# A two-layer encoder kernel: three places for expert tiles and four for gathered rows, in place of four and three

## What is computed

```python
def peer_ffn(h, w_query, sub_keys, expert_u, expert_v):     # 8 heads, 128 x 128 keys
    q = (xc @ w_query).reshape(PEER_CHUNK, PEER_HEADS, 2, PEER_HALF)
    sc = jnp.einsum('chpd,hpkd->chpk', q, sub_keys)
    ...                                   # top 16 of each half, then top 16 of the 256 pairs
    gate = jax.nn.softmax(top_s, axis=-1)
    u = jnp.take(expert_u, idx, axis=0)   # 128 experts for each token, 2048 floats each
    act = jax.nn.gelu(jnp.einsum('chkd,cd->chk', u, xc), approximate=False)
    vsel = jnp.take(expert_v, idx, axis=0)
    return jnp.einsum('chk,chkd->cd', (gate * act).astype(xc.dtype), vsel)
```

## Time and profile before

| | us |
|---|---|
| median of 3 runs | 3923.73 (3920.32 to 3927.78) |
| the profiled execution, its own time | 3927.2 |
| its span, first to last instruction | 3925.3 |
| TensorE busy | 3732.7 (95%) |
| VectorE busy | 2349.7 (60%) |
| GpSimd busy | 1168.9 (30%) |
| U tiles of the first layer | from 775.9 |
| V tiles of the first layer | 1389 to 1952 |
| U tiles of the second layer | from 2731 |
| V tiles of the second layer | 3345 to 3908 |

### The profile page before, as it was taken

One profiled execution on the slowest core, in us unless ns is written; L12 is line 12 of the kernel. 1 busy time (PEld: TensorE's weight loads), 2 busy tenths in 40 slices (PEclk: granted clock), 3 DMA queues, 4 the chain that ended last, 5 costly groups with the idle time before them and its releaser, 6 DMA issues. The chain is left out here.

```text
span 3925.3 us, 63110 instructions
## 1 busy us (share of the span) xinstructions
PE 3732.7 (95%) x26656; PEld 3403.6 (87%) x26656; DVE 2349.7 (60%) x4219; ACT 429.9 (11%) x1020; POOL 1168.9 (30%) x924
## 2 busy tenths in 40 slices
PE   7997889999999999999979978899999999999998
PEld 5786784799999899999967867747999998999998
DVE  5975752696388754444369657516953886544442
ACT  1013220110111000000010222101101110000000
POOL 2610000023133355455335100000331333555553
PEclk9998899999999999999989978999999999999999
DMA  5430013489899999999643300143998999999995
GB/s 160 139 119 10 2 45 134 141 340 405 334 397 396 392 368 357 373 349 372 241 138 130 118 10 2 45 160 129 359 399 336 398 397 390 379 364 368 349 359 228
DMA packets 305655, 994.14 MB, mean 253 GB/s; under 512 B 58861, under 2 KB 157549, under 8 KB 223917
## 3 DMA queue, kind: packets, MB, share of 16 engines
q0 software_dynamic: 118656, 587.71, 38.8%
q1 hardware_dynamic: 186720, 402.41, 28.0%
HBM read 1071.38 MB, written 2.10 MB: 273 GB/s over the span
## 5 line engine op out<-in xcount | busy, mean ns | idle before, releaser
L1679 PE MATMUL bank<-ycT,ex_tile 128*128 128x160 f32 x8192 | 1134.6, 300 | 0.0
L1679 PEld LDWEIGHTS bank<-ycT,ex_tile 128*128 128x128 f32 x8192 | 1119.9, 191 | 8.7 <-issue 8.4
L1752 PEld LDWEIGHTS bank<-ex_W,ex_tile 128*128 128x128 f32 x8192 | 1113.3, 190 | 6.7 <-issue 6.7
L1752 PE MATMUL bank<-ex_W,ex_tile 128*128 128x160 f32 x8192 | 1116.6, 299 | 0.0
L1618 POOL DMA_INDIRECT ex_row<-in_peer_u,ex_rows x240 | 260.5, 1085 | 1639.7 <-DVE ex_rows L1912 1191.8
L1954 DVE CUSTOM_DVE_ANT_0 ex_row<-ex_row,ex_h_wide 128x2048 f32<-128x2048 f32 x192 | 439.1, 2291 | 387.8 <-DMA ex_row<-in_peer_u,ex_rows 385.2
L1960 DVE SCALAR_TENSOR_TENSOR ex_sums<-ex_row,ex_weight,ex_sums 128x2048 f32<-128x2048 f32 x186 | 437.1, 2350 | 368.0 <-DMA ex_row<-in_peer_v,ex_rows 368.0
L336 PE MATMUL pj_bank<-pj_hT,pj_piece 128*128 128x256 f32 x2048 | 461.1, 384 | 5.9 <-DVE pj_hT L607 5.9
L1629 POOL DMA_INDIRECT ex_tile<-in_peer_v,ex_wanted x256 | 326.7, 1276 | 452.0 <-PE bank L1752 421.3
L336 PEld LDWEIGHTS pj_bank<-pj_hT,pj_piece 128*128 128x128 f32 x2048 | 389.6, 192 | 72.3 <-issue 13.8
L799 PE MATMUL bank<-arena,ycT 128*128 128x512 f32 x512 | 222.4, 593 | 2.0 <-PEq L884 2.0
(11 more groups left out here) (377 smaller groups left out, 3326.5 us busy)
## 6 DMA issues: line engine op xcount, KB each, us to landing
ex_tile<-in_peer_uT SPq DMA_DIRECT2D x256, 1024.0 KB, 8.1
pj_piece<-in_w_in SPq DMA_DIRECT2D x32, 2048.0 KB, 8.7
arena<-in_w_out SPq DMA_DIRECT2D x16, 2048.0 KB, 7.9
query_w<-in_peer_w_query SPq DMA_DIRECT2D x16, 1024.0 KB, 5.5
ex_row<-in_peer_u,ex_rows POOLq DMA_INDIRECT x312, 9.6
ex_row<-in_peer_v,ex_rows POOLq DMA_INDIRECT x256, 8.9
ex_tile<-in_peer_v,ex_wanted POOLq DMA_INDIRECT x256, 8.0
x<-in_x SPq DMA_DIRECT2D x1, 2048.0 KB, 8.8
```

What stands on the lines that cost most here:

```text
L1679: mm = mmul(o, ring[:, j % SLOTS, k * P:k * P + P], hT[k // 4][:, k % 4, 0:DENSE], start=(k == 0), stop=(k == KT - 1))
L1752: mm = mmul(bank[:, at_, lo:lo + DENSE], ring[:, i % SLOTS, m * P:m * P + P], W[:, j, :], start=(j == 0 and m % 3 == 0), stop=(j == TILES ...
```

## The change

One place moves from the ring of tiles to the ring of rows; the sum of both stays at seven, so all else in the on-chip memory lies where it lay. `FOLD_1_AT` moves by two.

```diff
-SLOTS = 4
-RING = 3
+SLOTS = 3
+RING = 4
-WIDEN_2, FOLD_1, FOLD_1_AT = 28, 64, 147
+WIDEN_2, FOLD_1, FOLD_1_AT = 28, 64, 149
```

## The result

| | before | after |
|---|---|---|
| median of 4 runs, us | 3925.8 (3920.3 to 3928.7) | 3996.7 (3988.2 to 4002.0) |
| profiled execution, its span | 3925.3 | 3993.0 |

The changed kernel takes 1.018 of the time before (95% interval 1.0168 to 1.0192), 71 us more by the medians. It is slower, as forecast, and the time lies inside the range, 1.3 us from its upper end, but the loss is more than twice the 33 us of the sum. One number further down needs a note: of ten runs of the kernel with VectorE's lists later, one took 15348 us; it has no trace, and the ratio leaves it out.

A forecast was written before the change was run, and what follows sets the result against it. TensorE was taken as the bound at 4.35 us a tile, DMA engines right behind. Terms V +30, U +5, turn +6, fold -8 sum to +33 us, forecast 3957 us; range 3930 to 3998.

The forecast's parts named there:

- the V term: V tiles of both layers: landings over 7.75 us make TensorE wait with three places; +30 us, between 0 and 81.
- its signs: Profile after: short L1752 waits, V stretch over 563 us, DMA share below 0.96, fold waits about 4 shorter, first V issue later.
- turn: From U to V tiles: v_tile(0) issued some 5 us later behind two more gathers; 3 us a layer, +6 together.
- fold: U tiles 114 to 117: fourth row place puts VectorE one row further ahead; 4 us a layer, -8 together.
- SyncE's loop: SyncE issuing U tiles in laps of three in place of four: some more branches, costing nothing.
- U tiles 0 to 61: U tiles with gathers: landings over the 8.30 us limit make TensorE wait; +5 us, range 0 to 12, both layers.
- U tiles 104 to 113 and 118 to 127: Late U tiles: 1.3 us from tile 104, taken in by the fold's wait, costing nothing unless that wait goes.
- (4.51 + issue + landing) / 3: Time per tile with three places, or 4.35 us if more; V landings up to 7.75 us cost nothing.
- the rival's half: First rival's fold part: fourth row lets VectorE reach the fold in time, winning all 21.7 us; whole rival 3902, chance 0.07.
- the first two rivals: Landings shrink under the limit: fold's wait goes, 3902 us, chance 0.07; or fold gives one turn, 3927 us, chance 0.08.
- The third: Four rows queue in front of a V tile, so landings grow by one us: 4065 us, chance 0.08.
- The fourth: Fourth place for rows never filled when it matters, so the -8 is missing: 3965 us, inside the forecast.

The follow-up runs named there:

- e1: Changed kernel with the fourth place for rows taken away (three places for tiles, three for rows): 4009.6 us, ratio 1.0212 to the kernel before.
- e2: Changed kernel with 92 in place of 94 gathers ahead of the first V tile: 3985.1 us, ratio 1.015 to the kernel before.
- e3: Changed kernel with gathers behind the 94th of a layer fetching only the first half of each row: 3962.3 us.
- e12: Kernel before (four places for tiles, three for rows), with VectorE serving no row at U tiles 106, 109 and 112: 3901.9 us, ratio 0.994.
- e9: Kernel before with 89 in place of 92 gathers ahead of the first V tile, fold where it was: 3944.0 us, ratio 1.0046.

## Why the prediction was right and wrong

The sign and the mechanism were right: three places for tiles do not hold the round trip. The sizes were not, and the largest miss is the V term, +30 where 50.5 us were measured. Most of its signs came as named: many waits at L1752 of under 3 us (the longest, 5.5, is the turn), a V stretch well over 563 us, a DMA share of 0.92 in place of 0.96, the first V issue 6.5 us later. Two did not: the waits do not stand at the ends of the V stretches, and the fold's wait isn't shorter by 4 us but gone. SyncE's loop costs nothing that can be seen, U tiles 62 to 103 take 220.1 us in both kernels; nor does `FOLD_1_AT`, since TensorE waits for VectorE at no fold in the V tiles. The terms, both layers together:

| term | predicted | measured |
|---|---|---|
| V tiles: waits and the slower tile behind each | +30 (0 to 81) | 42.0 + 8.5 = +50.5 |
| turn: the gap, and the slow first tile | +6 (0 to 12) | 10.7 + 4.7 = +15.4 |
| U tiles 0 to 61 | +5 (0 to 12) | 2.8 + 15.3 = +18.1 |
| U tiles 104 to 113 and 118 to 127 | 0 | 4.5 + 3.8 = +8.3 |
| fold | -8 (-21.7 to 0) | -23.3 |
| elsewhere | 0 | -1.3 |
| sum | +33 | +67.7 |

That the time still lies inside the range is in part luck: the U tiles and the turn went over their upper ends and the late U tiles over their 0, 17.8 us together, and the fold, 15.3 us better than forecast, paid most of that back.

**V tiles: mis-sized by the median.** The step that failed is "(4.51 + issue + landing) / 3" with a median put in. It holds for a steady landing. With scatter a landing over 7.75 us costs its whole excess, and a short one gives nothing back. By the rule above the landings of the *before* trace would have given 32.5 + 40.7 = 73 us where the medians gave 36. That is too much by the amount that the landings eased (means 7.9 and 8.1 us before, 7.5 and 7.5 after). The two errors worked against each other. The measured 50.5 lies between the 30 taken and the upper end of 81, whose own terms add up to 80. The reason for taking 30, that a waiting TensorE also asks for less, is real, but worth only about 0.5 us of landing. 46 waits with a median landing under the limit are the plain proof that the median can't price this.

**The tile behind a wait** was priced at the fold (2.15 us) and forgotten everywhere else. In after each V tile behind a wait takes 4.61 us in place of 4.51, and all of the slower V tiles but the first come to 8.5 us. The first V tile, behind 5 us of waiting, takes 6.8 and 6.9.

**U tiles: the same error**, and outside its bounds, which took the slower half of 47 tiles at its mean excess and again by a third. The named sign of it ("waits in U tiles 12 to 61 of more than 12 us in all") is just short of coming true as waits, 5.5 + 5.2, but the stretches grew by 15.3. The waits in the U tiles aren't scatter alone: tiles 11, 27, 39, 42 and 110 wait in both layers of after, e1 and e2 alike, so that what the program issues beside them, and not chance alone, makes the long landings there. The late U tiles cost 8.3: 104 to 113 because the wait that was to swallow them went, as the text had left open.

**The turn: the chain was right, its middle value wrong.** Gather 93 behind VectorE, v_tile(0) behind gather 93, at 1387.25 where "near 1386" was said; V tile 0 should then start at 1393.8 and started at 1395.86. Taken was the 3 of a range up to 6, for a VectorE that would be less late; but GpSimd still waited 3.73 us for it. The gaps, 10.7 us, are inside the range; with the slow first tile, which the sum forgot, the term is outside it. e2 shows it nearly by itself: 11.6 us between the two medians, while 1.9 us of the fold's wait are back.

**The fold: the rival's half came true inside the forecast.** "Worth one turn of 5.1 us" a layer, and then "the engines are full" so that nothing more can come. The whole wait went, with its slow tile 11.4 and 11.9 us. It did so for two reasons, which e1 takes apart: with three rows 6.9 of the 17.4 us went, with the fourth the other 10.5, which is the one turn of 5.1 us a layer that the prediction had named. The 6.9 us are in the main the tiles in front, which are later and give VectorE time, but only those from 104 on, 2.3 + 2.9 us in e1 up to tile 113. What U tiles 0 to 61 lose is no help, though it is some 8 us a layer: VectorE is in step with the tiles up to 103, where in before it waits 32 times for ScalarE's part of a tile (21.9 us between U tiles 62 and 103). The remaining 1.7 us are not explained, and no run has four rows beside four tiles. The sum had the delay of the late U tiles and the fold's wait as independent terms; they are not.

**The rivals.** Landings did shrink, by 0.5 us, and with two places they go on shrinking (6.3). The median even went under the 7.75 us that the first two rivals ask for, and TensorE waited all the same, because single landings go up to 10.7 us: both fall. In those sentences the rule of the Trainium skill, DMA: Bandwidth & Descriptors, anatomy of one DMA on the GpSimd path (4.4 us for 1 MB as an estimate), stood as their price. The trace disagrees with it as a price under load: 7.5 us with whole rows beside, 6.7 with half rows; only the shortest come near it, 4.9 us in after and 4.3 in e3. And a V tile moves less than 1 MB: of the 587.71 MB on GpSimd's queue in before, 384 gathers of 1.05 MB leave 185 MB for 256 V tiles, 0.72 MB for each. The third, landings of 9 and more, falls too: four rows queued no longer than three, and the gathers behind V tiles now wait for no place at all. The fourth, that the fourth place is never filled, falls by e1, 13 us slower without it.

The e12 kernel answers what the rivals only priced: 21.7 us were to be had at the fold, and 24 were won (23.3 of them in the stretch of the fold), by asking for fewer rows there and leaving the tiles their four places.

## What to carry to other kernels

To price a ring with one place fewer, take the landings one by one, not their median: the limit is places x period - use - issue, each landing over it costs its whole excess less the waits of the places - 1 tiles before it, and each wait also slows the tile behind it. With the landings of the deeper ring this is an upper price (73 us against 42 here), since landings ease. When a consumer waits for an engine that is late in one stretch, look for the work which that engine was *asked* to do there and could do later, before giving it more buffers or moving the place where it is met; moving the meeting point only moves the wait to the next gate. Terms that lie one after another on the path are not independent: a delay ahead of a wait is paid out of the wait, but only where the engine that is waited for is already behind and can use the time.

## What the hardware showed that was not expected

- In after a tile behind even a short wait takes 4.61 us in place of 4.51, at a granted clock of 1.00 over the stretch. Behind a longer one the clock is lower: after the 4.83 us at 1395.86 the 6.7 us of the first V tile show a granted clock of 0.66, a mixture of the two levels 1.2 and 2.4 GHz, and the next stretch 1.00 again. The same shows in e9 behind 6.72 us of waiting for ScalarE, where hardly a transfer runs (DMA share 0.01), so it isn't the transfers. The border between the two isn't sharp: behind after's longest other wait, 2.04 us, a tile takes 4.61 us, but behind waits of 1.87 and 1.92 us in e1 it takes 6.29 (granted clock 0.73), and behind one of 2.58 us in e2 6.12 (0.75). Of after, then of e9, in the columns of the earlier trace rows:

```profile
1395.90:1402.60 6.70, 6.70 (x33) 6.70 (x34) 6.49 (x12) 0.00 (x0) 2.20 (x2) 0.66 0.95 352
1403.00:1410.00 7.00, 7.00 (x53) 7.00 (x53) 3.48 (x5) 0.74 (x2) 4.15 (x4) 1.00 0.67 241
```

```profile
1397.50:1404.00 6.50, 6.50 (x33) 6.50 (x34) 2.54 (x3) 0.00 (x0) 1.37 (x2) 0.67 0.01 3
```

- The landing of a V tile depends on how many are in flight (means 8.0, 7.5 and 6.3 us with four, three and two places; with half rows beside it hardly, 6.8 and 6.7 with four and three) and on the bytes of the gathers beside it (7.5 with whole rows and three places, 6.7 with half rows). Its scatter stays: even at a DMA share of 0.74 the longest is 9.4 us. What makes single landings of V tiles that long was not found.
